# Attention ordered by blocks, with projections ending at steps and the softmax division at the outputs

## The chip, the core and the metric

The kernel runs on one core of a Trainium2 chip. The metric is the device time of one execution, in microseconds, as the median of several.

## What is computed

Two transformer blocks over 1024 tokens of width 1024: one with an mLSTM and pooling mixer and a mixture of experts, one with forgetting attention and a multilayer perceptron. The change touches the attention of the second alone:

```python
def fox_mixer(h, w_in, b_f, q_g, k_g, w_out):
    proj = h @ w_in
    q, k, v, f_pre = jnp.split(proj, [D, 2 * D, 3 * D], axis=-1)
    q = rms_norm_2(q.reshape(B, S, 16, 64), q_g)
    k = rms_norm_2(k.reshape(B, S, 16, 64), k_g)
    F = jnp.cumsum(log_sigmoid(f_pre + b_f), axis=1)
    logits = q @ k * 64 ** -0.5 + (F[t] - F[s])      # s <= t
    p = jax.nn.softmax(logits, axis=-1)
    return (p @ v) @ w_out
```

All in f32. A product that must be exact is made of three matmuls with high and low halves (`split_mm`, lines 1622 to 1624).

## The kernel before

`build` runs phases one behind the other, each a block in which every engine has a written instruction stream and semaphores join them. The phases are mixer, experts, `attention`, `fox_out` and `mlp`. In `attention` the 16 heads are done as 8 pairs. For a pair TensorE projects the normed input to q, k and v in 8 tiles of 128 tokens (`project`, bank 4, eight k of three matmuls each). Two tiles make a batch of q and k: ACT copies the rows (`rows_out`) and squares them, DVE sums (`sums`), POOL makes the root (`root`, L1905 and L1907), DVE scales (`normed`, L2162), TensorE turns (`turn_batch`, L2003), ACT and DVE split into high and low (`high_batch`, L2081 to L2083; `low_batch`, L2171 and L2173).

A head has four groups n of 256 queries, with g = n % 4; group g sees 2g + 2 tiles of keys, in g + 1 blocks b of two. For a group: `logits` on TensorE (L1958 to L1960, banks 0 to 3), `forgotten` on DVE adds the forget sums and takes the row minimum (L2130), `exp` on ACT with the row sum (L2039), `share` on POOL: reciprocal of the row sum (L1912) and the whole probabilities times it (L1914). For each block TensorE turns the probabilities (`turn_probs`, L1975, banks 5 and 6 in turn), ACT copies the high half (L2048), DVE subtracts for the low half (L2137), and TensorE weighs v with both (`weigh`, L1991 and L1992, bank 7, whose two halves serve groups in turn). `copy_out` on ACT (L2056) and `add_out` on DVE (L2144) put the output together; SP stores it once per pair (L1888).

The streams are loops over slots, one group to a slot, written by hand. In slot n TensorE makes the logits of group n + 1 and the turning and weighing of group n, with pieces of the projection of tile n + 8 between:

```python
for n in slots:
    logits(n + 1, 0); project(n, (0, 1))
    logits(n + 1, 1); project(n, (2, 3))
    turn_probs(n, 0); project(n, (4,))
    for b in range(g + 1):
        if b < g:
            turn_probs(n, b + 1); project(n, (5 + b,))
        elif g < 3: project(n, range(5 + g, KT))
        weigh(n, b)
    if batch_in(n) is not None: turn_batch(batch_in(n))
```

Eight slots before group 0 have projections alone (the fill). The banks 5 and 6 alternate over blocks and batches in the order of turning (`z_block`, `z_batch`), and a turning waits until ACT and DVE have left its bank. The weights of a pair are loaded in two halves into one tile `w_qkv` (L1864, three DMAs each); each is split by ACT (`high_weights`, L2034) and DVE (`low_weights`, L2118), and SP loads a half only when the low split of the one before is done. In the last slot of a pair ACT does one `high_weights` behind the first turned block and the other at the slot's end.

## Time and profile before

| | |
|---|---|
| median of 3 executions | 3104.9 us (3104.64 to 3107.49) |
| profiled execution | 3103.1 us, span 3101.4 us |
| busy, share of the span | PE 83%, PEld 68%, DVE 60%, ACT 40%, POOL 18% |
| mean granted TensorE clock | 0.899 |
| attention | from 1540 to 2251 us of the span |
| L1991, weighing with the high half | 81.1 us idle before it, 80.7 of them for L2137 |
| L2048, high half of the turned probabilities | 29.6 and 35.3 us idle before its two forms |

Times are of one profiled execution. PE is the matrix engine (TensorE), PEld its weight loads, DVE VectorE, ACT ScalarE, POOL GpSimd, SP the engine that issues DMAs. A clock of 1.0 is 2.4 GHz. Ends of matmuls are modelled and they overlap, so the time that a matmul takes is read from the start of it to the start of the next.

### The profile page before, as it was taken

How to read it: one execution, taken by the hardware profiler on the slowest of the kernel's cores; microseconds unless marked ns; L12 is line 12 of the kernel's file. 1: busy time of each engine (PE TensorE's matmuls, PEld its weight loads, DVE VectorE, ACT ScalarE, POOL GpSimd, SP SyncE). 2: the span in 40 equal slices, each digit the busy share in tenths (PEclk: the TensorE clock that was granted, in tenths of full speed). 3: DMA queues.
4: the chain of work that ended last, by engine and by line, in shares of the span. 5: the costliest groups of instructions: out<-in, count | busy, mean ns of one | idle time of the engine just before them, and what ended most of it. 6: DMA issues, size and time to landing. Idle time of an engine off the chain costs nothing. (4 is left out here: it accounts for less than half of the span.)

```text
span 3101.4 us, 34604 instructions
## 1 busy us (share of the span) xinstructions
PE 2564.8 (83%) x12069; PEld 2116.0 (68%) x12069; DVE 1848.8 (60%) x2460; ACT 1250.9 (40%) x1817; POOL 563.9 (18%) x609
## 2 busy tenths in 40 slices
PE   3998767556999999981478888888685999999999
PEld 2766456455887888870377777777564888888887
DVE  6873693355888888875435555555445445554554
ACT  2212531105777777772245555555422121112111
POOL 1000020111111111104225555555400000000000
PEclk8999758757999999995599999999796999999999
DMA  5683233417968799985111110110042111111111
GB/s 210 220 291 111 96 122 102 158 42 304 393 269 318 289 390 399 398 326 217 55 52 42 41 35 31 41 31 32 7 176 68 41 54 54 41 54 41 54 54 55
DMA packets 137677, 443.01 MB, mean 143 GB/s; under 512 B 15134, under 2 KB 74050, under 8 KB 124264
## 3 DMA queue, kind: packets, MB, share of 16 engines
q1 hardware_dynamic: 124140, 394.97, 34.7%
q0 software_dynamic: 8144, 27.80, 2.5%
q10 hardware_dynamic: 5292, 18.94, 1.5%
q8 instruction: 58, 0.95, 0.1%
q14 instruction: 43, 0.35, 0.0%
HBM read 384.91 MB, written 56.76 MB: 142 GB/s over the span
## 5 line engine op out<-in xcount | busy, mean ns | idle before, releaser
L1622 PE MATMUL psum<-w_high,block_hT_high 128*128 128x512 f32 x576 | 233.4, 405 | 22.8 <-DVE w_low L1328 18.0
L2428 DVE TENSOR_TENSOR x<-x,psum 128x512 f32<-128x512 f32 x256 | 172.8, 685 | 112.4 <-PE psum L1624 112.4
L1622 PE MATMUL psum<-w_qkv_high,fox_hT_high 128*128 128x384 f32 x512 | 199.8, 390 | 34.5 <-DVE w_qkv_low L2118 25.0
L1623 PE MATMUL psum<-w_low,block_hT_high 128*128 128x512 f32 x576 | 226.7, 393 | 0.0
L1624 PE MATMUL psum<-w_high,block_hT_low 128*128 128x512 f32 x576 | 226.4, 393 | 0.0
L1328 DVE TENSOR_TENSOR w_low<-w_up,w_high 128x2048 fp32r<-128x2048 f32 x72 | 161.7, 2288 | 90.0 <-ACT w_high L1322 90.0
L1622 PE MATMUL psum<-hT_high,w_mlp_in_high 128*128 128x512 f32 x512 | 200.1, 391 | 7.1 <-DVE w_mlp_in_low L2405 7.1
L1623 PE MATMUL psum<-hT_low,w_mlp_in_high 128*128 128x512 f32 x512 | 199.9, 390 | 0.0
L1624 PE MATMUL psum<-hT_high,w_mlp_in_low 128*128 128x512 f32 x512 | 199.7, 390 | 0.0
L1622 PE MATMUL psum<-w_mlp_out_high,hiddenT_high 128*128 128x512 f32 x512 | 199.2, 389 | 0.0
L1623 PE MATMUL psum<-w_mlp_out_low,hiddenT_high 128*128 128x512 f32 x512 | 199.2, 389 | 0.0
L1624 PE MATMUL psum<-w_mlp_out_high,hiddenT_low 128*128 128x512 f32 x512 | 199.2, 389 | 0.0
L1328 DVE TENSOR_TENSOR w_low<-w_gate,w_high 128x2048 fp32r<-128x2048 f32 x72 | 164.3, 2284 | 40.0 <-ACT w_high L1322 39.9
L2137 DVE TENSOR_TENSOR probsT_low<-psum,probsT_high 128x512 fp32r<-128x512 f32 (+1 forms) x160 | 98.9, 634 | 135.6 <-ACT probsT_high L2048 135.0
L1623 PE MATMUL psum<-w_qkv_low,fox_hT_high 128*128 128x384 f32 x512 | 176.8, 345 | 0.0
L1624 PE MATMUL psum<-w_qkv_high,fox_hT_low 128*128 128x384 f32 x512 | 176.6, 345 | 0.0
L1322 ACT ACTIVATE w_high<-w_gate 128x2048 fp32r<-128x2048 f32 x72 | 137.5, 1913 | 91.9 <-DMA w_gate<-in_w_expert_gate 84.2
L1991 PE MATMUL psum<-probsT_high,v_high_low 128*128 128x256 f32 x320 | 96.6, 321 | 81.1 <-DVE probsT_low L2137 80.7
L1328 DVE TENSOR_TENSOR w_low<-w_down,w_high 128x2048 fp32r<-128x2048 f32 x72 | 161.5, 2282 | 3.5 <-ACT w_high L1322 3.5
L2416 DVE TENSOR_TENSOR relu_squared<-relu 128x512 f32<-128x512 f32 x64 | 44.2, 691 | 194.2 <-ACT relu L2384 194.2
L2379 ACT ACTIVATE w_mlp_out_high<-w_mlp_out 128x2048 fp32r<-128x2048 f32 x16 | 30.7, 1917 | 319.0 <-DVE w_mlp_out L2409 319.0
L1622 PEld LDWEIGHTS psum<-w_high,block_hT_high 128*128 128x128 f32 x576 | 109.7, 190 | 58.9 <-DVE w_low L1328 32.5
(402 smaller groups left out, 6704.7 us busy)
## 6 DMA issues: line engine op xcount, KB each, us to landing
w_gate<-in_w_expert_gate SPq DMA_DIRECT2D x32, 2048.0 KB
w_up<-in_w_expert_up SPq DMA_DIRECT2D x32, 2048.0 KB, 9.1
w_down<-in_w_expert_down SPq DMA_DIRECT2D x32, 2048.0 KB, 10.4
v_aug<-in_w_ada SPq DMA_DIRECT2D x48, 512.0 KB, 4.8
expert_rows<-block_out ACTq DMA_DIRECT2D x36, 512.0 KB, 9.1
v_aug<-in_ada_w SPq DMA_DIRECT2D x32, 512.0 KB, 4.7
expert_rows<-work SPq DMA_DIRECT2D x1, 16384.0 KB, 44.1
w_mlp_in<-in_w_mlp_in SPq DMA_DIRECT2D x16, 1024.0 KB, 5.1
```

The source lines that it names most:

```text
L1322: act.activation(wh[:, par, half], raw[kind][:, half], ACT.Copy).then_inc(s_wh, 1)
L1328: dve.tensor_tensor(wl[:, par, half], raw[kind][:, half], wh[:, par, half].bitcast(F32), ALU.subtract).then_inc(s_wl, 1)
L1622: pe.matmul(out, sh, mh, start=start, stop=False)
L1623: pe.matmul(out, sh, ml, start=False, stop=False)
L1624: return pe.matmul(out, sl, mh, start=False, stop=stop)
L1991: pe.matmul(out_, v, pTh[:, y % 2, at], start=s == 0, stop=False)
L2137: dve.tensor_tensor(pTl[:, y % 2, 0:width], bank[5 + z % 2][:, 0:width], pTh[:, y % 2, 0:width].bitcast(F32), ALU.subtract).then_inc(s_lo, 1)
L2379: act.activation(w2h[:], w2[:], ACT.Copy).then_inc(s_w2h, 1)
L2416: dve.tensor_tensor(gf[:, g % 2, :], rl[:, g % 2, :], rl[:, g % 2, :], ALU.mult).then_inc(s_sq, 1)
L2428: dve.tensor_tensor(x3[:, t, at], x3[:, t, at], bank[4 + j % 4], ALU.add).then_inc(s_r, 1)
```

## The change

The streams are now loops over steps, one block to a step: 20 steps of fill and 160 blocks. In step y TensorE turns block y + 1, makes the logits of the group whose first block is y + 4, runs a share of a projection, and weighs block y. A pair's 8 tiles are cut into 18 shares of 2 to 4 k, such that a tile ends with a step; steps 18 and 19 of a pair have none. A batch whose second tile ends in step c is turned at the end of step c + 2 and split in step c + 3. Both halves of the next weights are split in step 18. The names with changed lines: logits L1988 to L1990, `turn_probs` L2009, `weigh` L2024 and L2025, `turn_batch` L2037, `high_weights` L2060, `exp` L2065, `high_probs` L2074, `copy_out` L2081, `rows_out` L2088, `high_batch` L2105 to L2107, `low_weights` L2137, `forgotten` L2149, `low_probs` L2156, `add_out` L2162 and L2164, `low_batch` L2190 and L2192.

The probabilities stay undivided. POOL makes a 128x128 diagonal of reciprocals per query tile; one matmul of ones with the two diagonals (L2029) spreads them over the partitions in the second half of bank 7, and DVE multiplies the finished output by it. The first half of bank 7 serves all groups, so a group's first weighing waits for the output before it. The semaphores are counted apart for blocks and batches, and each g has a probabilities tile of its own.

```diff
-            pe_ = sbuf(c2, "probs_even", [P, 5 * P + 6 * P])
-            po_ = sbuf(c2, "probs_odd", [P, 7 * P + 8 * P])
+            pb = [sbuf(c2, f"probs{g}", [P, (4 * g + 3) * P]) for g in range(4)]
+            dg = sbuf(c2, "recip_diagonal", [P, 2, 2 * P])
...
+            STEPS = 20
+            AHEAD = 4
+            BUSY = 18
+            parts = ((0, 4, 8), (0, 4, 8), (0, 3, 6, 8), (0, 4, 8), (0, 4, 8), (0, 3, 6, 8), (0, 4, 8), (0, 4, 8))
+            blocks = [(n, b) for n in range(NG) for b in range(n % QUADS + 1)]
...
                     def share(j):
...
-                        pool.tensor_scalar(probs(n, u), probs(n, u), rs[:, j % 4:j % 4 + 1], None, ALU.mult).then_inc(s_p, 1)
+                        if n >= 2 and u == 0:
+                            pool.wait_ge(s_rb, n - 1)
+                        pool.tensor_scalar(dg[:, n % 2, u * P:(u + 1) * P], ident[:], rs[:, j % 8:j % 8 + 1], None, ALU.mult).then_inc(s_dg, 1)
+                    for y in steps:
+                        if batch_at(y - 1) is not None:
+                            root(batch_at(y - 1))
+                        if group_at(y - 1) is not None:
+                            for u in range(2):
+                                share(2 * group_at(y - 1) + u)
...
+                    def bank_left(z):
+                        if z >= 2:
+                            kind, at = holds[z - 2]
+                            pe.wait_ge(s_hi if kind == "block" else s_bh, at + 1)
+                            pe.wait_ge(s_lo if kind == "block" else s_bl, at + 1)
...
                     def weigh(n, b):
-                        if b == 0 and n >= 2:
-                            pe.wait_ge(s_o, n - 1)
-                        pe.wait_ge(s_lo, z_block[n, b] + 1)
+                        if b == 0 and n >= 1:
+                            pe.wait_ge(s_o, n)
+                        pe.wait_ge(s_lo, y + 1)
...
+                        if b == g:
+                            pe.wait_ge(s_dg, 2 * n + 2)
+                            pe.matmul(bank[7][:, 2 * P:HALF], ones[:], dg[:, n % 2, :], start=True, stop=True).then_inc(s_rb, 1)
...
+                    for y in steps:
+                        if 0 <= y + 1 < NY:
+                            turn_probs(*blocks[y + 1])
+                        if group_at(y) is not None:
+                            logits(group_at(y), 0)
+                            logits(group_at(y), 1)
+                        for q, k in products_at(y):
+                            project(q, k)
+                        if y >= 0:
+                            weigh(*blocks[y])
+                        if batch_at(y - 2) is not None:
+                            turn_batch(batch_at(y - 2))
...
+                    for y in steps:
+                        if 0 <= y + 1 < NY:
+                            high_probs(*blocks[y + 1])
+                        if left_at(y) is not None:
+                            copy_out(left_at(y))
+                        if group_at(y - 1) is not None:
+                            exp(2 * group_at(y - 1))
+                            exp(2 * group_at(y - 1) + 1)
+                        if batch_at(y - 3) is not None:
+                            high_batch(batch_at(y - 3))
+                        if y % STEPS == BUSY and y // STEPS + 2 < PAIRS:
+                            high_weights(2 * (y // STEPS + 2))
+                            high_weights(2 * (y // STEPS + 2) + 1)
+                        if tile_at(y) is not None:
+                            rows_out(tile_at(y))
+                        if batch_at(y) is not None:
+                            square(batch_at(y))
...
                     def add_out(n):
-                        dve.tensor_tensor(o[rows[h], at], o[rows[h], at], bank[7][rows[h], half:half + 2 * P], ALU.add).then_inc(s_o, 1)
+                        dve.tensor_tensor(o[rows[h], at], o[rows[h], at], bank[7][rows[h], 0:2 * P], ALU.add).then_inc(s_oa, 1)
+                        dve.wait_ge(s_oa, n + 1)
+                        dve.tensor_tensor(o[rows[h], at], o[rows[h], at], bank[7][rows[h], 2 * P:HALF], ALU.mult).then_inc(s_o, 1)
...
+                    for y in steps:
+                        if 0 <= y + 1 < NY:
+                            low_probs(*blocks[y + 1])
+                        if left_at(y) is not None:
+                            add_out(left_at(y))
+                        if batch_at(y - 2) is not None:
+                            normed(batch_at(y - 2))
+                        if group_at(y) is not None:
+                            forgotten(2 * group_at(y))
+                            forgotten(2 * group_at(y) + 1)
+                        if batch_at(y - 1) is not None:
+                            sums(batch_at(y - 1))
+                        if batch_at(y - 3) is not None:
+                            low_batch(batch_at(y - 3))
+                        if y % STEPS == BUSY and y // STEPS + 2 < PAIRS:
+                            low_weights(2 * (y // STEPS + 2))
+                            low_weights(2 * (y // STEPS + 2) + 1)
+                        if tile_at(y) is not None:
+                            v_low(tile_at(y))
```

The order on TensorE where a batch has been turned, in the first pair: the reciprocals (`recip_diagonal`) and the batch (`qk_rows`) at the end of step 5, then step 6 with a turned block, the logits of a small group and the first k of the projection.

```order
L2029 MATMUL psum<-recip_diagonal,ones 128x256
L2037 MATMUL psum<-ident,qk_rows 128x128 x4
L2009 MATMUL psum<-ident,probs 128x128 x4
L1988 MATMUL psum<-k_high_twice,q_stacked 128x128
L1989 MATMUL psum<-k_low,q_stacked 128x128
L1990 MATMUL psum<-causal_bf,ident_bf 128x128
L1988 MATMUL psum<-k_high_twice,q_stacked 128x256
L1989 MATMUL psum<-k_low,q_stacked 128x256
L1990 MATMUL psum<-causal_bf,ident_bf 128x128
L1622 MATMUL psum<-w_qkv_high,fox_hT_high 128x384
L1623 MATMUL psum<-w_qkv_low,fox_hT_high 128x384
L1624 MATMUL psum<-w_qkv_high,fox_hT_low 128x384
```

One more k follows here and one weighing; then the next block is turned, into the batch's bank. Before, a whole slot's projection of eight k stood around two turnings.

The order on ACT at the weights of a pair, before, in the last slot of the pair before it (`w_qkv_high` is the high split):

```order
L2048 ACTIVATE probsT_high<-psum 128x512
L2034 ACTIVATE w_qkv_high<-w_qkv 128x1536
L2039 ACTIVATE probs_even,row_sum<-probs_even,row_min 128x256
L2048 ACTIVATE probsT_high<-psum 128x512 x2
L2048 ACTIVATE probsT_high<-psum 128x384
L2064 ACTIVATE qk_rows<-psum 128x256
L2065 ACTIVATE v_high_low<-psum 128x2x64
L2072 ACTIVATE qk_square<-qk_rows 128x512
L2034 ACTIVATE w_qkv_high<-w_qkv 128x1536
L2056 ACTIVATE outT<-psum 64x256
```

and now, in steps 18 and 19:

```order
L2065 ACTIVATE probs,row_sum<-probs,row_min 128x384
L2065 ACTIVATE probs,row_sum<-probs,row_min 128x512
L2060 ACTIVATE w_qkv_high<-w_qkv 128x1536 x2
L2074 ACTIVATE probsT_high<-psum 128x384
L2074 ACTIVATE probsT_high<-psum 128x512
L2081 ACTIVATE outT<-psum 64x256
L2065 ACTIVATE probs,row_sum<-probs,row_min 128x640
L2065 ACTIVATE probs,row_sum<-probs,row_min 128x768
```

The two splits were seven instructions apart and now are one row with x2; the copies of turned blocks stand behind both.

The order on DVE at the same place, before (`w_qkv_low` is the low split, `qk_rows` the scaling of a batch):

```order
L2137 TENSOR_TENSOR probsT_low<-psum,probsT_high 128x512
L2118 TENSOR_TENSOR w_qkv_low<-w_qkv,w_qkv_high 128x1536
L2130 ISA probs_even,row_min<-psum,forget_sums 128x256
L2130 ISA row_min 128x1
L2137 TENSOR_TENSOR probsT_low<-psum,probsT_high 128x512 x2
L2137 TENSOR_TENSOR probsT_low<-psum,probsT_high 128x384
L2151 TENSOR_TENSOR v_high_low<-psum,v_high_low 128x128
L2118 TENSOR_TENSOR w_qkv_low<-w_qkv,w_qkv_high 128x1536
L2130 ISA probs_odd,row_min<-psum,forget_sums 128x384
```

and now:

```order
L2156 TENSOR_TENSOR probsT_low<-psum,probsT_high 128x384
L2176 TENSOR_REDUCE qk_sums<-qk_square 128x8
L2137 TENSOR_TENSOR w_qkv_low<-w_qkv,w_qkv_high 128x1536 x2
L2156 TENSOR_TENSOR probsT_low<-psum,probsT_high 128x384
L2181 TENSOR_TENSOR qk_rows<-qk_rows,qk_sums 128x512
L2149 ISA probs,row_min<-psum,forget_sums 128x640
L2149 ISA row_min 128x1
```

Both low splits stand in one row, ahead of a turned block's subtraction and the scaling of the batch that TensorE turns at the end of step 19.

## Rows read from the trace of the kernel before

**Rows 1.** two stretches of attention; us, busy us per engine (instructions), clock, DMA share, GB/s
```profile
1776.40:1858.10 81.70, 70.46 (x434) 62.27 (x433) 45.09 (x95) 46.26 (x107) 44.03 (x40) 0.98 0.13 40
2181.60:2250.70 69.10, 45.47 (x205) 36.82 (x205) 29.09 (x61) 27.98 (x62) 35.89 (x30) 0.68 0.02 8
```

**Rows 2.** waits of TensorE in attention: us in total, times, longest
```profile
PE psum L1991 <- DVE probsT_low L2137: 80.7, 68, 2.8
PE psum L1975 <- DVE k_low L2173: 11.8, 13, 1.2
PE psum L1975 <- POOL probs_odd L1914: 1.7, 2, 1.2
```

**Rows 3.** TensorE in order of time in steady pairs: start, us, instruction
```profile
1861.51 0.47 PE L1958 MATMUL psum<-k_high_twice,q_stacked 128*128 128x512 f32 x1
...
1862.27 0.42 PE L1622 MATMUL psum<-w_qkv_high,fox_hT_high 128*128 128x384 f32 x1
...
1888.75 0.36 PE L1991 MATMUL psum<-probsT_high,v_high_low 128*128 128x256 f32 x1
...
1889.30 0.60 PE L1975 MATMUL psum<-ident,probs_odd 128*128 128x128 f32 x4
1889.65 0.42 PE L1622 MATMUL psum<-w_qkv_high,fox_hT_high 128*128 128x384 f32 x1
```

**Rows 4.** TensorE in order of time in the mixer, matmuls in plain f32
```profile
310.86 1.88 PE L549 MATMUL psum<-ucT,wq 128*128 128x512 f32 x4
312.58 1.88 PE L549 MATMUL psum<-ucT,wk 128*128 128x512 f32 x4
```

**Rows 5.** groups of instructions in attention: count, busy us, mean ns, idle before
```profile
L2137 DVE TENSOR_TENSOR probsT_low<-psum,probsT_high 128x512 fp32r<-128x512 f32 x96 | 64.7, 687 | 77.4 <-ACT probsT_high L2048 77.0
L2048 ACT ACTIVATE probsT_high<-psum 128x512 fp32r<-128x512 f32 x96 | 55.0, 589 | 29.6 <-PE psum L1975 29.4
L1907 POOL TENSOR_TENSOR qk_sums<-qk_sums,minus_half 128x8 f32<-128x8 f32 x32 | 53.6, 1674 | 2.7
L2171 DVE SCALAR_TENSOR_TENSOR q_stacked<-psum,qk_gain,q_stacked 64x256 fp32r<-64x256 f32 x64 | 30.9, 483 | 48.6 <-ACT k_high_twice L2083 48.2
L2081 ACT ACTIVATE q_stacked<-psum,qk_gain 64x256 fp32r<-64x256 f32 x64 | 30.1, 470 | 18.8 <-PE psum L2003 17.5
L2144 DVE TENSOR_TENSOR outT<-outT,psum 64x256 f32<-64x256 f32 x64 | 26.7, 417 | 4.1 <-ACT outT L2056 3.2
L2056 ACT ACTIVATE outT<-psum 64x256 f32<-64x256 f32 x64 | 24.1, 376 | 19.1 <-PE psum L1992 18.6
L2162 DVE TENSOR_TENSOR qk_rows<-qk_rows,qk_sums 128x512 f32<-128x512 f32 x32 | 22.0, 689 | 12.0 <-POOL qk_sums L1907 12.0
L2157 DVE TENSOR_REDUCE qk_sums<-qk_square 128x8 f32<-128x512 f32 x32 | 21.7, 679 | 1.4 <-ACT qk_square L2072 1.0
```

**Rows 6.** all engines in order of time, weights at the fill's end
```profile
1599.19 1.47 ACT L2034 ACTIVATE w_qkv_high<-w_qkv 128x1536 fp32r<-128x1536 f32 x1
...
1600.70 1.76 DVE L2118 TENSOR_TENSOR w_qkv_low<-w_qkv,w_qkv_high 128x1536 fp32r<-128x1536 f32 x1 [1.21 <-ACT w_qkv_high L2034]
1602.48 0.37 SPq L1864 DMA_DIRECT2D w_qkv<-in_fox_w_in  x1
...
1607.51 1.48 ACT L2034 ACTIVATE w_qkv_high<-w_qkv 128x1536 fp32r<-128x1536 f32 x1 [2.85 <-DMA w_qkv<-in_fox_w_in]
...
1609.02 1.76 DVE L2118 TENSOR_TENSOR w_qkv_low<-w_qkv,w_qkv_high 128x1536 fp32r<-128x1536 f32 x1 [4.56 <-ACT w_qkv_high L2034]
```

**Rows 7.** TensorE in order of time behind the fill
```profile
1600.38 0.23 PE L1960 MATMUL psum<-causal_bf,ident_bf 128*128 128x128 bf16 x1
1604.56 0.66 PE L1622 MATMUL psum<-w_qkv_high,fox_hT_high 128*128 128x384 f32 x1 [3.94 <-DVE v_high_low L2151]
...
1609.31 0.52 PE L1624 MATMUL psum<-w_qkv_high,fox_hT_low 128*128 128x384 f32 x1
...
1611.12 0.34 PE L1623 MATMUL psum<-w_qkv_low,fox_hT_high 128*128 128x384 f32 x1
```

More of the change, by code:

```diff
@@ L1842, in where, with group_at, left_at, products_at @@
                 return i, r // QUADS, r % QUADS
+            def group_at(y):
+                n, b = blocks[y + AHEAD] if 0 <= y + AHEAD < NY else (None, 1)
+                return n if b == 0 else None
+            def left_at(y):
+                n, b = blocks[y - 1] if y >= 1 else (None, None)
+                return n if n is not None and b == n % QUADS else None
+            def products_at(y):
+                i, c = y // STEPS + 1, y % STEPS
+                if i >= PAIRS or c >= BUSY:
+                    return []
+                t, ks = shares[c]
+                return [(TT * i + t, k) for k in ks]
+            def tile_at(y):
+                done = [q for q, k in products_at(y) if k == KT - 1]
+                return done[0] if done else None
+            def batch_at(y):
+                q = tile_at(y) if y >= -STEPS else None
+                return q // 2 if q is not None and q % 2 == 1 else None
+            z_block, z_batch = {}, {}
+            for y in steps:
+                if 0 <= y + 1 < NY:
+                    z_block[blocks[y + 1]] = len(z_block) + len(z_batch)
+                if batch_at(y - 2) is not None:
+                    z_batch[batch_at(y - 2)] = len(z_block) + len(z_batch)
+            holds = {z: ("block", y_block[nb]) for nb, z in z_block.items()} | {z: ("batch", m) for m, z in z_batch.items()}
             def probs(n, u):
                 g = n % QUADS
-                buf = po_ if g % 2 else pe_
-                width = (2 * g + 1 + u) * P
-                start = 0 if u == 0 else (7 * P if g % 2 else 5 * P)
-                return buf[:, start:start + width]
-            def batch_in(n):
-                return (n + 6) // 2 if n % 2 == 0 and 0 <= (n + 6) // 2 < NB else None
+                start = 0 if u == 0 else (2 * g + 1) * P
+                return pb[g][:, start:start + (2 * g + 1 + u) * P]
             with nc.Block() as block:
@@ L2125, in forgotten @@
                             dve.wait_ge(s_f[h], 16 * (i + 1))
[L2126 to L2127 removed]
+                        if n >= QUADS and u == 0:
+                            dve.wait_ge(s_t, z_block[n - QUADS, g] + 1)
                         dve.wait_ge(s_lg, j + 1)
```

169 lines of the change are left out of this document (41 added, 128 removed).

## The prediction

> **What bounds the kernel now.** I read the stretches of attention by head pair first [rows 1], then the waits of TensorE [rows 2], then single instructions. Attention is a stage of its own, whose last output is stored at 2250.7 us. A pair of heads takes 81.7 us and TensorE counts as busy for 70.5 of them, at a granted clock of 0.98. DVE and ACT are busy for 45 to 46, POOL for 44. So TensorE is the bound, and what it loses is waiting: 80.7 us for the low half of the turned probabilities in the whole stage, 11.8 for the low half of a batch of q and k, only 1.7 for POOL's division [rows 2]. In the last pair, which has no projections left to fill gaps, TensorE works little (clock 0.68) and the pair still takes 69.1 us [rows 1].
>
> TensorE's true work in a pair comes from starts, since busy time includes pipeline tails [rows 3]: four turned tiles 0.35 us (1889.30 to 1889.65), a weighing of four matmuls 0.55 (1888.75 to 1889.30), one chunk of logits with its mask 0.76 (1861.51 to 1862.27). One k of a projection is three matmuls at 0.17, so 0.52. A pair has 64 k (33.3), 88 transposes (7.7), 80 weighing matmuls (8.3 with the narrow ones), logits of 9.9, and 0.1 for each switch between kinds (3.8): 63 us. The other 18.7 of the 81.7 are waits.
>
> **The change, part by part.** *Removed:* POOL's pass over the probabilities. It stood on TensorE's path for 1.7 us [rows 2], so its end is worth almost nothing in the first seven pairs; in the last one it is in the chain of every group. *Added:* one matmul of 256 columns in plain f32 per group. Such matmuls show as two records each; four records, two matmuls of 512 columns, start 1.72 us before the next four [rows 4], so 0.86 for 512 columns and 0.43 for 256. With a switch I take 0.5, 8 per pair: 4 us, and TensorE's work becomes 67. The bounds are 0.43 and, at half clock, 0.95. DVE gets a second 0.42 us operation per group on the outputs [rows 5]: 3.4 us per pair on an engine with 36 free, but in the chain below. POOL's new 128x128 products are off the path.
>
> *Moved:* the order. Turned probabilities are now weighed a whole step later, with a projection between; a chain of copy 0.59 and subtraction 0.69 [rows 5] fits under that. The 80.7 us of waits go, as meant. What is late next are four other waits; I walked the 20 steps of a pair, with E the end of its last projection.
>
> 1. *Weights, once per pair.* ACT now makes the two high halves of the next weights one behind the other, and so does DVE with the low halves (the order on ACT and on DVE). They share one staging tile: the second half is loaded only after the first has been subtracted. The trace has this chain once, at the end of the fill [rows 6]: high copy at 1599.19, low at 1600.70, load issued at 1602.48, second high copy at 1607.51 after 2.85 us idle. That is 8.3 us from copy to copy, and the second low ends 3.3 later. Before, a slot's work stood between the two. Now ACT starts at E+3.0 (seven instructions stand ahead, at the mean of 0.43 us that 46.26 us for 107 give [rows 1]), the second high copy starts at E+11.3 and DVE is free at E+14.6. Behind it on DVE stand one subtraction and the scaling of the last batch, 1.3 us together. TensorE needs that scaled batch at E+4.0, after 3.5 us of other work in the two steps without projection, and gets it at E+15.9: 11.9 us.
>
> 2. *Batches, four per pair.* The two banks for turning alternate, so the second turning after a batch waits for the batch's bank. In the step between, ACT does a probabilities copy 0.59, an output copy 0.38 and six batch copies of 0.47, then DVE four of 0.48 [rows 5]: with 0.6 for the turning itself it ends 6.3 us after the step began. TensorE's work in those steps is 2.5 to 3.6 (the order on TensorE shows the shortest: 2 k, two small logits). So it waits 3 us, four times: 12.1. The nearest row is L1975 waiting 11.8 us in 13 waits for the same DVE line [rows 2]: there several pieces of projection stood between.
>
> 3. *Outputs.* One half bank is left for a group's output (the other holds the reciprocals), so the next group's first weighing waits for the store of the last: after the turning 0.3, copy 0.59, subtraction 0.69, add and multiply 0.84, some 2.5 us, against 1.1 to 2.2 of projection. Over eight groups 3.6 us.
>
> 4. *Small ones:* a projection tile that waits for the last one's copies behind a long step (0.8 and 0.9), a batch whose root (1.67 us [rows 5]) is queued on POOL behind a reciprocal that waits for an output (0.85), and one more (0.35): 2.9 us.
>
> A pair: 67 + 11.9 + 12.1 + 3.6 + 2.9 = 97.5. After the long wait TensorE runs slow: following 3.94 us idle the matmuls took 0.52 us in place of 0.34 from 1604.56 to past 1609.31 [rows 7], five microseconds that do the work of half as many, so up to 2.5 lost, part of it under wait 2. I add 2: a period of 99.5.
>
> *The sum.* Before, the fill's last matmul starts at 1600.4 [rows 7], and the end is at 2250.7: 650.3 us. After, the fill is the same, seven sets of weights each open a pair's period, and the last pair runs alone. It keeps 12 steps of 1.3 us (half the copy, subtraction and weighing chain), eight handovers of 3.7, 10 of logits that partly show, and one batch wait, 62 us; with some of it at half clock, as now (0.68), I take 66. So 7 x 99.5 + 66 = 762.5, 112 more than 650.3. The profiled execution took 3103.1 us (span 3101.4); its median is 3104.9, 1.8 higher, and I carry that along: **3217 us**.
>
> The Trainium skill (DMA: Bandwidth & Descriptors, Anatomy of one DMA) states about 2.0 us fixed plus bytes over 436 GB/s. For the 786 KB of one half of the weights that gives an estimate of 3.8 us, where the rows have 5.0 from first issue to the copy; by the page each pair would be 1.2 us shorter, 3209 in all. The measured load decides.
>
> **Rivals.**
>
> *Projections stay the bound, and it is faster.* The new order hides all the chains, and a pair is its work of 67 plus 3.6 at the outputs: 7 x 70.6 + 62 = 556, 94 less, **3011**. For it speaks that 80.7 us of waits have no place left; against it that in the order the paired weights and the bank's return stand where nothing covers them. It decides at a period of (650.3 - 66) / 7 = 83.5: all waits of a pair under 16.5 us, where I count 30.5. Chance 0.06.
>
> *The weights' load is covered.* If the second half is ready when ACT asks, 8.3 us shrink to some 1.5, seven times: 48 less, **3169**. For it: three loads of one half land quickly at times; against: the tile is single, and the load waits for DVE. Chance 0.08.
>
> *The clock falls at each wait.* If the 3 us waits lower TensorE's clock as the 3.94 us one did [rows 7], four per pair lose up to 2.5 each, less the 2 already counted: 7 x 8 = 56 more, **3273**. Against it: waits up to 2.8 us [rows 2] left the clock of a pair at 0.98 [rows 1]. Chance 0.07.
> The Trainium skill (TensorE: Matmul & The Clock Gate, HAM oscillation) states that a wait for data between bursts makes the array start each burst at the low clock; that is this rival, and it speaks against the change. The trace agrees for 3.94 us and not for 2.8.
>
> *It moves waits and nothing more:* the new waits come to the old ones, a period of 83.5, **3105**. Chance 0.03.
>
> **How the numbers follow.** My forecast has 0.76. A measurement of this kernel tells 0.2%, 6 us, from no change. The range: the nearest large uncertainties are the start of the weights chain (1 us per pair), the waits for batches (2.3 to 3.5 us each, 5 per pair) and the clock (0 to 5 per pair), together about minus 45 and plus 50 around 3217; it takes in the covered load and reaches to the clock's rival: 3150 to 3268. Outside are the faster case, the equal one and half of the clock's, 0.13. Faster by over 0.2%: 0.06. Within: 0.03. Slower: 0.76 + 0.08 + 0.07 = 0.91.
>
> **What would show it.** The waits of the weighing (L2024) for the low half near 0 outside the last pair; the turning of batches (L2037) waiting some 12 us, once per pair, for the scaling on DVE; ACT idle 3 to 5 us before each second weights copy for its DMA; L2009 waiting about 3 us for DVE's k_low, four times a pair; stores of outputs 97 to 102 us apart. I am wrong if the stores are under 84 us apart, or if L2037's waits are short: then the weights were hidden. A granted clock under 0.85 in a full pair would be the clock's rival.

## The result and the profile after

The changed kernel takes **3273.9 us** (median of 4, 3269.0 to 3279.4) against 3105.0 on the same chip: a ratio of 1.0543, 95% interval 1.0522 to 1.0563. The profiled execution took 3269.0 us (span 3267.2). The forecast was slower, 3217; the time lies 57 us above it, 6 above the range.

All of it is in attention, which ends at 2418.2 in place of 2250.7. What follows it is 850 us long in both traces. A full pair and the last one, in the columns of [rows 1]:

```profile
1946.09:2052.46 106.37, 78.17 (x442) 70.79 (x442) 48.42 (x102) 45.80 (x107) 27.07 (x41) 0.87 0.10 30
2360.50:2418.20 57.70, 37.48 (x203) 30.43 (x203) 27.64 (x58) 24.45 (x54) 13.70 (x24) 0.80 0.03 10
```

A pair grew from 81.7 to 106.4 us. TensorE's busy time grew by 7.7 and its granted clock fell from 0.98 to 0.87; DVE and ACT do what they did, POOL does 17 us less. The waits of TensorE in attention (us in total, times, longest), which stand against [rows 2]:

```profile
PE psum L2037 <- DVE qk_rows L2181: 89.5, 16, 12.9
PE psum L2009 <- DVE k_low L2192: 67.6, 22, 4.1
PE psum L2024 <- DVE outT L2164: 32.5, 29, 2.3
PE psum L2009 <- issue: 20.2, 7, 2.9
PE psum L1622 <- ACT qk_rows L2088: 17.8, 19, 1.1
...
PE psum L2024 <- DVE probsT_low L2156: 0.9, 3, 0.3
```

The 80.7 us for the low half are 0.9 now, as meant; in their place stand 210 us for batches, banks and outputs. The long wait is the weights' chain, here in all engines' order of time (against [rows 6]):

```profile
2032.80 0.33 PE L1624 MATMUL psum<-w_qkv_high,fox_hT_low 128*128 128x384 f32 x1
...
2035.81 1.48 ACT L2060 ACTIVATE w_qkv_high<-w_qkv 128x1536 fp32r<-128x1536 f32 x1
2037.33 1.76 DVE L2137 TENSOR_TENSOR w_qkv_low<-w_qkv,w_qkv_high 128x1536 fp32r<-128x1536 f32 x1 [1.52 <-ACT w_qkv_high L2060]
...
2043.73 1.48 ACT L2060 ACTIVATE w_qkv_high<-w_qkv 128x1536 fp32r<-128x1536 f32 x1 [6.44 <-DMA w_qkv<-in_fox_w_in]
2045.25 1.76 DVE L2137 TENSOR_TENSOR w_qkv_low<-w_qkv,w_qkv_high 128x1536 fp32r<-128x1536 f32 x1 [6.16 <-ACT w_qkv_high L2060]
2047.39 0.68 DVE L2181 TENSOR_TENSOR qk_rows<-qk_rows,qk_sums 128x512 f32<-128x512 f32 x1
```

From E = 2032.8: the copies start at E+3.0 and E+10.9, and TensorE goes on at 2048.22, E+15.4, after 11.01 us. The sum had 3.0, 11.3 and 15.9. What the sum had not is in the first and third of these windows of the pair, right behind two of the waits for a batch's bank (3.30 and 2.88 us long); the second stands behind one of 2.94 us:

```profile
1951.40:1956.60 5.20, 5.20 (x19) 5.20 (x20) 1.29 (x3) 1.35 (x4) 0.00 (x0) 0.50 0.00 0
1979.00:1984.00 5.00, 4.94 (x32) 4.53 (x33) 2.01 (x6) 1.91 (x6) 2.29 (x4) 1.00 0.00 0
2002.70:2007.70 5.00, 5.00 (x16) 3.79 (x17) 2.12 (x4) 0.60 (x1) 0.00 (x0) 0.50 0.00 0
```

At 0.50 (1.2 GHz) TensorE does 16 to 19 matmuls in 5 us, at 1.00 (2.4 GHz) 32. This pair is the exception: in the other five pairs before the last, the clock falls behind all four waits for a batch's bank. In the pair before this one, two windows behind the waits of 2.95 and 2.63 us:

```profile
1871.50:1874.80 3.30, 3.30 (x12) 2.78 (x11) 1.77 (x5) 1.31 (x5) 2.18 (x4) 0.50 0.02 5
1919.30:1926.00 6.70, 6.17 (x21) 5.37 (x22) 2.25 (x6) 1.59 (x5) 2.29 (x4) 0.50 0.00 0
```

I multiplied the busy time of every microsecond of a pair by one minus its clock, and call it the lost work: 9.2 us in the pair from 1946 to 2052 (7.9 to 10.1 in the five pairs that have the long wait), and 1.7 in each of four pairs of before. There the clock falls once a pair, behind a wait of some 2.0 us, while a longer one in the same pair leaves it high (kernel before; the waits, then the windows behind them):

```profile
2001.10 0.38 PE L1991 MATMUL psum<-probsT_high,v_high_low 128*128 128x256 f32 x1 [1.96 <-DVE probsT_low L2137]
2014.06 0.38 PE L1991 MATMUL psum<-probsT_high,v_high_low 128*128 128x256 f32 x1 [2.80 <-DVE probsT_low L2137]
```

```profile
2002.70:2006.00 3.30, 3.30 (x15) 3.30 (x15) 0.59 (x3) 2.49 (x8) 0.80 (x1) 0.50 0.00 0
2014.10:2018.10 4.00, 3.81 (x26) 3.46 (x27) 1.35 (x3) 2.90 (x5) 0.38 (x1) 1.00 0.46 128
```

### The profile page after: what moved, and what is told of

Same layout as the page of the kernel before. It is cut to its first block and busy times, and to the rows that moved or that the text cites. A ratio compares the mean times of both kernels' runs of the same rounds, so it can differ in the third digit from the quotient of the medians.

```text
span 3267.2 us, 34985 instructions
## 1 busy us (share of the span) xinstructions
PE 2616.3 (80%) x12197; PEld 2171.6 (66%) x12197; DVE 1877.1 (57%) x2524; ACT 1251.2 (38%) x1817; POOL 424.2 (13%) x609
## 5 line engine op out<-in xcount | busy, mean ns | idle before, releaser
L2156 DVE TENSOR_TENSOR probsT_low<-psum,probsT_high 128x512 fp32r<-128x512 f32 (+1 forms) x160 | 102.0, 638 | 239.1 <-ACT probsT_high L2074 239.1
L2074 ACT ACTIVATE probsT_high<-psum 128x512 fp32r<-128x512 f32 (+1 forms) x160 | 88.8, 555 | 361.4 <-PE psum L2009 361.3
L1623 PE MATMUL psum<-w_qkv_low,fox_hT_high 128*128 128x384 f32 x512 | 185.7, 363 | 0.0
L1624 PE MATMUL psum<-w_qkv_high,fox_hT_low 128*128 128x384 f32 x512 | 184.3, 360 | 0.0
L2009 PE MATMUL psum<-ident,probs 128*128 128x128 f32 x576 | 102.6, 302 | 87.7 <-DVE k_low L2192 67.6
```

The source lines that it names most:

```text
L1623: pe.matmul(out, sh, ml, start=False, stop=False)
L1624: return pe.matmul(out, sl, mh, start=False, stop=stop)
L2009: ins = pe.transpose(bank[5 + z % 2][:, at:at + P], probs(n, u)[:, s * P:(s + 1) * P], ident[:])
L2074: act.activation(pTh[:, y % 2, 0:width], bank[5 + z % 2][:, 0:width], ACT.Copy).then_inc(s_hi, 1)
L2156: dve.tensor_tensor(pTl[:, y % 2, 0:width], bank[5 + z % 2][:, 0:width], pTh[:, y % 2, 0:width].bitcast(F32), ALU.subtract).then_inc(s_lo, 1)
```

## The experiments

Ratios are to the kernel before on the same chip, us differences are ratio differences times 3104.

| run | ratio (95%) | against the changed kernel |
|---|---|---|
| changed kernel | 1.0543 (1.0522 to 1.0563) | |
| e1 weights split | 1.0320 (1.0303 to 1.0337) | -69 |
| e2 late | 1.0142 (1.0125 to 1.0159) | -124 |
| e3 filler in the long wait | 1.0535 (1.0517 to 1.0552) | -2 |
| e4 no division | 1.0455 (1.0435 to 1.0475) | -27 |
| e5 order alone | 1.0658 (1.0640 to 1.0676) | +36 |
| e6 division alone | 1.0104 (1.0086 to 1.0121) | -136 |
| e7 = e1 and e2 | 1.0070 (1.0053 to 1.0087) | -147 |
| e8 = e7, old division | 1.0079 (1.0061 to 1.0097) | -144 |
| e9 filler, misplaced | 1.1008 (1.0983 to 1.1032) | +144 |
| e10 second half later | 1.0167 (1.0145 to 1.0190) | -117 |
| e11 transposes late only | 1.0953 (1.0927 to 1.0979) | +127 |
| e12 filler at two banks | 1.0536 (1.0519 to 1.0554) | -2 |
| e13 copies first only | 1.0268 (1.0251 to 1.0285) | -85 |
| e14 = e7, scaling early | 1.0053 (1.0035 to 1.0071) | -152 |
| e15 = e1 and e13 | 1.0193 (1.0168 to 1.0218) | -109 |
| e16 better order | **0.9823 (0.9810 to 0.9837)** | -223 |
| e17 = e16, old division | 0.9889 (0.9874 to 0.9905) | -203 |
| e18 = e14, two stores | 0.9993 (0.9984 to 1.0003) | -171 |

**e1, the weights' halves in two steps** (ACT, and the same on DVE):

```diff
-if y % STEPS == BUSY and y // STEPS + 2 < PAIRS:
-    high_weights(2 * (y // STEPS + 2))
-    high_weights(2 * (y // STEPS + 2) + 1)
+if y % STEPS in (17, 19) and y // STEPS + 2 < PAIRS:
+    high_weights(2 * (y // STEPS + 2) + y % STEPS // 19)
```

> One thing is changed: the two halves of a pair's weights are copied and split in steps 17 and 19 of a pair instead of both in step 18, so the second half's load, which starts when the first half has been subtracted, lies beside a step and a half of other work. Theory (the long wait of TensorE once a pair, 12.9 us on qk_rows in the changed kernel, is ScalarE standing 6.7 us for that load and the two copies behind each other): the wait for DMA at the weights' copy falls from 6.7 us to under 1, TensorE's wait once a pair from 12.9 to 2 to 4 us, seven pairs, so about 60 to 70 us less with what the clock gives back: 3274 becomes about 3208. Rival (the long wait hides other waits, which appear in its place: the batch's chain of square, sums, root and product is as long by itself): TensorE still waits 8 us or more in step 19, and the time falls by under 30 us, to 3245 or more.

3201.1 us, 69 less. The waits in e1's trace:

```profile
PE psum L2009 <- DVE k_low L2191: 63.0, 22, 3.8
PE psum L2024 <- DVE outT L2163: 42.1, 35, 2.3
PE psum L2037 <- DVE qk_rows L2180: 23.0, 16, 4.0
```

The wait for scaled batches fell by 66.5 us, the outputs' rose by 9.6. ScalarE still waits for the load, 14.7 us in all in place of 45.7, so 2.1 each time where under 1 was expected. The theory holds, with its size: 9.5 us of TensorE's wait per pair came from copying and splitting both halves in one step; ScalarE's own wait for the load is 4.4 us shorter.

The pairs of e1 also show what the clock costs. TensorE has the same instructions in each and stands still for 19.8 to 20.1 us; these three lose 8.5, 6.4 and 10.0 us of work:

```profile
1713.23:1810.66 97.43, 77.63 (x440) 69.45 (x440) 48.56 (x102) 45.56 (x107) 27.48 (x40) 0.89 0.11 33
1810.66:1906.35 95.69, 75.62 (x440) 67.61 (x440) 48.52 (x102) 45.70 (x107) 27.48 (x40) 0.93 0.11 34
1906.35:2005.11 98.76, 78.95 (x440) 70.47 (x440) 48.42 (x102) 45.80 (x107) 27.49 (x40) 0.88 0.11 33
```

Between the second and the third the lost work grows by 3.6 us and the pair by 3.1: nearly all of it is paid for.

**e2, the order inside a step.** On PE:

```diff
 for y in steps:
-    if 0 <= y + 1 < NY:
-        turn_probs(*blocks[y + 1])
     ... logits, project ...
+    if 0 <= y + 1 < NY:
+        turn_probs(*blocks[y + 1])
     if y >= 0:
         weigh(*blocks[y])
```

and on ACT and DVE `high_probs` and `low_probs` move from the front of a step to behind output, exp (`forgotten`), batch and rows; the weights come last.

> The order inside a step is changed and no instruction added or taken away: TensorE issues logits and projections ahead of the transposes of the next block, and ScalarE and VectorE take batch and output work ahead of the block's copy. Theory (the four waits of about 3 us a pair on k_low and the waits for outT come from transposes that stand at the front of a step and need a bank that the batch's copies still hold; with matmuls ahead of them they are covered): those waits fall from 67.6 us and 32.5 us in all to under 20 and 10, the stretches at half clock that follow them go too, and the time falls by 80 to 140 us, to about 3135 to 3195, with the long wait for weights left as it is. Rival (the waits only change place, since ScalarE and VectorE are then late with the block's copies, which weigh needs in the same step): waits at the matmuls on probsT_low take their place and the time stays within 20 us of 3274 or rises.

124 us less. The waits on k_low fell from 67.6 us (22 times) to 2.7 (once), those of the outputs to 7.9. The waits for scaled batches rose by 20, to 109.8 us. The expectation holds. All waits of TensorE in attention together fell by some 70 us, and the work lost at half clock from about 9 to 1.4 to 3.0 us a pair, some 50 us in all: together nearly the 124. So the lost work is paid for here.

**e13 and e11, its two halves.** e13 has the edits on ACT and DVE alone, e11 the one on PE alone.

> The other half of the order inside a step: ScalarE and VectorE do output, exp and batch ahead of the next block's copy, TensorE keeps the changed kernel's order with the transposes in front. Theory (the bank wait is the batch's copies standing behind the block's copy; taking them first frees the bank and the outputs about 1.3 us earlier): the waits on k_low fall from 67.6 us by a third to a half and those on outT from 32.5 to about 10, 40 to 80 us less: 3195 to 3235. Rival (both halves are needed together, since the block's copy is now late for the weighing in the same step): as slow as 3274 or slower, with waits of the weighing on probsT_low.

> Half of the earlier run of the order inside a step: only TensorE's order is changed, logits and projections ahead of the next block's transposes; ScalarE and VectorE keep the changed kernel's order, the block's copy first. Theory (what was saved there, 127 us, came from TensorE having work to do before it needs the bank): most of it, 80 us or more, so 3195 or less. Rival (ScalarE and VectorE now stand at the block's copy, which comes later, and do the batch behind it, so the bank comes free later too): less than 40 us, 3235 or more.

e13 took 3183.3 us, 85 less, more than the 40 to 80 expected: the waits on k_low fell from 67.6 to 19.9 us. (Its edit on DVE also moves the scaling of a batch behind `forgotten`, as e2's does.) e11 took 3394.7, 127 **more**. Alone, the late transposes are waited for by ACT at the front of its step, with the last group's output behind them, so TensorE waits for the output in nearly every group (e11's trace):

```profile
PE psum L2024 <- DVE outT L2164: 130.9, 58, 3.6
```

The rival of e11 (3235 or more) was right in its number but named the wrong wait (k_low is 9.9 there). The two halves are no sum: -85 and +127 give -124 together. An order on three engines is one thing.

**e3, filler in the long wait.**

```diff
+if y % STEPS == STEPS - 1 and y // STEPS + 2 < PAIRS:
+    pe.wait_ge(s_raw, TT * (y // STEPS + 2))
+    pe.wait_ge(s_vl, TT * (y // STEPS + 2))
+    for _ in range(56):
+        pe.matmul(bank[4][:, 0:W3], hTh[:, 0, 0:P], hTh[:, 0, 0:W3], start=True, stop=True)
```

> 56 matmuls of 128x384 whose result nobody reads are added once a pair, in step 19 in front of the batch's transposes, where TensorE stands for about 11 us; they are about 9 us of work at full clock and end before what TensorE waits for there. Theory (part of the change's cost is that the clock falls to half at such a wait and the matmuls behind it run slowly): with the wait filled, the work behind it runs at full clock, and the kernel becomes 1.5 to 4 us a pair faster though it does more: about 3248 to 3264. Rival (the clock's share is nothing that this wait causes): the time stays at 3274 within 4 us, or rises.

3268.8 us, no difference. The trace is of an execution of 3282.3 us, the slowest of the four. The filler filled the wait and the clock held behind it (first row), but the next turning waits for its bank whatever TensorE does: 4.10 us, where the changed kernel has 3.30 to 4.06, and it starts 5.3 us after the pair's store in both kernels. Behind the later waits the clock fell as it does in most pairs of the changed kernel, and stayed low for longer: a pair loses 10.8 to 12.5 us. The second row is behind the wait of 2.62 us (3.1 us lost); the changed kernel lost as much there in one pair, 1.4 to 1.5 in four, and held the clock in one (the row by itself):

```profile
1944.90:1947.90 3.00, 2.79 (x19) 2.47 (x17) 2.57 (x7) 2.29 (x5) 0.31 (x1) 1.00 0.82 238
1922.60:1928.60 6.00, 6.00 (x21) 5.17 (x22) 1.86 (x5) 1.59 (x5) 2.29 (x4) 0.50 0.00 0
```

```profile
2029.30:2035.30 6.00, 5.95 (x42) 5.46 (x42) 2.71 (x8) 3.71 (x12) 2.30 (x4) 1.00 0.00 0
```

**e9, filler at the short waits, misplaced.**

```diff
+if batch_at(y - 3) is not None and y >= 0 and y % STEPS != 6:
+    done = sum(1 for x in range(-STEPS, y) if tile_at(x) is not None)
+    pe.wait_ge(s_raw, done)
+    pe.wait_ge(s_vl, done)
+    for _ in range(40):
+        pe.matmul(bank[4][:, W3:HALF], hTh[:, 0, 0:P], hTh[:, 0, 0:P], start=True, stop=True)
```

> The changed kernel with 40 matmuls of 128x128 that nobody reads put where TensorE waits some 3 us for a batch's bank, in three of the four places of a pair (in the fourth a projection tile is open in bank 4); about 2.3 us of work each at full clock. In the changed kernel TensorE is busy at half clock for 9.2 us of lost work a pair, most of it right behind these waits, and only 1.7 in the kernel before. Theory (the 7 us a pair that the sum missed are that lost work): with the clock held, 3 to 6 us a pair come back though work is added, so 3230 to 3255, ratio about 1.045. Rival (as in the run with filler in the long wait, what TensorE does faster it waits longer for at the next bank): 3268 or more, ratio 1.052 or more.

144 us more. It tests nothing of the theory: it is the second turning after a batch that waits for its bank, and the filler stood ahead of the first, where nothing is waited for. It was also twice as long as the 2.3 us that I had put for it, a third of the 0.17 of a 128x384 matmul each:

```profile
2080.90 4.66 PE L2046 MATMUL psum<-fox_hT_high 128*128 128x128 f32 x40
```

**e12, filler where the waits are.**

```diff
+if y >= 0 and y % STEPS in (1, 12):
+    pe.wait_ge(s_add, 2 * sum(1 for x in range(-STEPS, y) if group_at(x) is not None))
+    for _ in range(20):
+        pe.matmul(bank[1][:, 0:2 * P], hTh[:, 0, 0:P], hTh[:, 0, 0:2 * P], start=True, stop=True)
```

> The run before put its filler one turning too early, where TensorE does not wait, and its 128x128 matmuls start only every 0.117 us, so it was added work and no test. Here 20 matmuls of 128x256 (0.117 us each, 2.3 us) stand directly in front of the two turnings, in steps 1 and 12 of a pair, at which the changed kernel waits 3.3 and 2.9 us and after which the clock is at half for 5 to 6 us. Theory (the 7 us a pair that the sum missed are TensorE's work at half clock behind such waits): with the clock held there, 3 to 5 us a pair less, 3240 to 3255, ratio 1.044 to 1.048. Rival (what is done faster is waited for at the next bank, as in the run with filler in the long wait): 3266 or more, ratio 1.052 or more.

3267.3 us, no difference, so the rival's number; but not by its mechanism. The filler stood where it should, and the clock behind the two waits is full (windows of e12, first and third row; the changed kernel falls to 0.50 at both, in every pair):

```profile
1949.30:1954.30 5.00, 5.00 (x31) 4.54 (x32) 2.28 (x6) 2.02 (x5) 0.00 (x0) 1.00 0.00 0
1974.60:1979.60 5.00, 5.00 (x17) 4.17 (x18) 2.03 (x6) 1.58 (x5) 2.29 (x4) 0.50 0.00 0
2000.90:2005.90 5.00, 4.95 (x30) 4.27 (x31) 2.84 (x5) 0.60 (x1) 0.00 (x0) 1.00 0.00 0
2011.40:2014.60 3.20, 3.20 (x13) 3.20 (x12) 0.92 (x2) 0.00 (x0) 1.87 (x2) 0.50 0.02 5
2025.20:2028.20 3.00, 3.00 (x11) 2.17 (x12) 1.20 (x4) 1.58 (x5) 0.61 (x2) 0.50 0.00 0
```

Counted from the pair's store, the next bank's wait ends at 30.6 us in place of 32.0 to 33.0, and the wait behind the second filler ends at 64.8 in place of 66.5 to 67.5. So some 2 us come back at each: the lost work is paid for, not covered. But the clock now stays low twice as long behind the wait of 2.93 us (second row, 3.0 us lost in place of mostly 1.7), and falls in every pair behind one of 1.28 us that had left it high in all pairs but one (fourth row, 1.7 us lost). So a pair still loses 7.9 us and takes 105.8, the same as the pairs of the changed kernel that lose 7.9 and 8.0 (105.8 and 106.0). Holding the clock at some of the waits made it fall for longer at others, and the theory's 3 to 5 us never came free to be measured.

**e4, e5 and e6, the two parts of the change apart.** e4 leaves out the division by the row sums (part of the computation), e5 is the new order with the old division, e6 the old order with the new one. Their common edit, out in e4 and e5 and in in e6:

```diff
 ins.then_inc(s_pv, 1)
-if b == g:
-    pe.wait_ge(s_dg, 2 * n + 2)
-    pe.matmul(bank[7][:, 2 * P:HALF], ones[:], dg[:, n % 2, :], start=True, stop=True).then_inc(s_rb, 1)
```

> The division by the row sums is left out altogether: the diagonals on GpSimd, the matmul of ones with them and VectorE's product with its result are gone, and ScalarE's copy of the output waits for the last product with v instead. Theory: per pair 8 matmuls in float32 of about 0.5 us go (4 us), and the waits for outT (32.5 us in all) shrink by half, so 40 to 55 us less: about 3220 to 3235. Rival (what the division's matmul and product cost is covered by the other waits): the time falls by under 15 us.

> The changed kernel with the old division: GpSimd multiplies the probabilities again, the turning waits for that, and the diagonals, the matmul of ones and VectorE's second product are gone. So it is the new order of steps by itself. Theory (the order costs nearly all of the 169 us, by the weights' chain, the batches' banks and the slow clock; the division moved to the outputs costs about 4 us a pair): 3235 to 3250, near the 3242 that the kernel without any division took, since GpSimd works four blocks ahead. Rival (GpSimd's pass over the probabilities is on the path in this order): above 3255, with waits of the transposes for GpSimd.

> The kernel before with only the division moved: reciprocals as diagonals on GpSimd, one matmul of 256 columns with ones per group, the product on the outputs, and so one half of bank 7 for outputs in place of two; the order of the slots is the old one. Theory: TensorE gets 4 us more work a pair, 32 in all, and waits for the outputs of the last group that the second half of the bank used to cover; the last pair gets shorter by GpSimd's passes: 3105 plus 32 plus 10 to 30 less 5 to 10, about 3130 to 3160. Rival (it is the division that costs most): above 3200. Other rival (it gains by itself): 3105 or less.

e4 3242.2, e5 3307.8, e6 3135.6 us: e4 is 7 us above its range, e5 at its rival, e6 in its range. Without a division the new order costs 141 us (1.0455). The division at the outputs adds 27 to that, on GpSimd it adds 63: in the new order GpSimd's pass **is** on the path, with a wait that the changed kernel has not (e5's trace):

```profile
PE psum L2007 <- DVE k_low L2185: 97.8, 29, 4.6
PE psum L2032 <- DVE qk_rows L2174: 83.8, 15, 11.6
PE psum L2007 <- POOL probs L1948: 40.2, 17, 5.0
```

In the old order the new division costs 32 us, near the 8 matmuls of 0.5 us a pair; TensorE's busy time less the lost work of a full pair is 64.4 to 64.9 us in e4 and 68.3 to 69.3 in the changed kernel. So the two parts don't add: order alone +204, division alone +32, both +169.

**e7, e8, e10, e14, e15, e18: towards an order without these waits.** e7 is e1 and e2 together, e8 the same with the old division, e15 is e1 and e13 together.

> The two edits of the runs before this one together: weights in steps 17 and 19, and the transposes behind logits and projections with the batch and output work first. Theory (the two costs are separate): 3144 less the long wait's 9 to 10 us a pair, seven times, 3075 to 3090, faster than the kernel before (3105), with the granted clock of a pair at 0.95 or more. Rival (in the other order the batch's chain of square, sums, root and product fills that wait anyway): over 3110, with waits of 8 us or more of the batch's transposes for the scaling.

> The same with the old division on GpSimd, no matmul of ones. Theory: 4 us of TensorE's work a pair less and shorter chains at the outputs: 25 to 40 us under the run with the new division, about 3040 to 3060, so the division at the outputs is a loss in a good order too. Rival (with the transposes late, GpSimd's pass is on the path): equal to that run or slower.

> The run with copies first on ScalarE and VectorE and transposes in front on TensorE, with the weights split in steps 17 and 19. Theory: that run less about 60 to 70 us, since the long wait goes as it did alone (73 us less) and in the first combination by less. Rival (as in the first combination, part of the long wait stays): only 20 to 40 us less.

e7 3122.1, e8 3126.7 (not to be told apart), e15 3159.1 us. After e2 the split gave 22 us, after e13 23, alone 69. The rivals of all three were nearer in number, but the wait of 8 us that e7's rival named is not there (2.3 us in its steady pairs). I had taken the two costs as separate; why the split gives less in the better orders is not shown. e8's division on GpSimd gained none of the 25 to 40 us expected.

e10 and e14 are built on e7. Both scale a batch earlier on DVE and have three diagonals; e10 also moves the second half of the weights to the next pair's first step.

```diff
-if y % STEPS in (17, 19) and y // STEPS + 2 < PAIRS:
-    high_weights(2 * (y // STEPS + 2) + y % STEPS // 19)
+if y % STEPS == 17 and y // STEPS + 2 < PAIRS:
+    high_weights(2 * (y // STEPS + 2))
+if y > 0 - STEPS and y % STEPS == 0 and y // STEPS + 1 < PAIRS:
+    high_weights(2 * (y // STEPS + 1) + 1)
```

> Built on the run that split the weights and put the transposes late: the second half of the weights goes to the first step of the next pair, VectorE scales a batch as its second task of a step instead of its fourth, and the diagonals have three buffers, so that GpSimd's root does not stand behind a diagonal that waits for an output. In that run TensorE still waited 46.5 us for scaled batches, GpSimd 64.7 us for the matmul of ones and ScalarE 4.5 us a pair for the load. Theory (these are one chain): the waits for scaled batches fall under 20 us and a pair from 85 to 80 or 82 us, so 3085 to 3105, level with the kernel before or under it. Rival (other waits come up behind): 3115 or more.

> The run with weights split in steps 17 and 19 and everything late (3122), with VectorE's scaling moved up and three diagonals, the weights left in steps 17 and 19. Theory (in the run before it was the second half of the weights in the next pair's first step that cost 6 us of waits a pair, and the scaling and the diagonals help): 3090 to 3115. Rival (scaling earlier only delays the row minimum behind it): 3122 within 6.

e10 was worse (3152.3, where 3085 to 3105 was expected): the projection of the next pair waits for the low half, some 3 us in most pairs, with others behind it. e14 took 3116.1, just above its range (3090 to 3115) and in its rival's (3122 within 6); its interval overlaps e7's, so its two edits are not shown to help. In e14's trace ScalarE still waits for two transfers:

```profile
ACT w_qkv_high L2060 <- DMA w_qkv<-in_fox_w_in: 32.1, 7, 4.8
...
ACT outT L2081 <- DMA heads_outputs<-outT: 14.3, 5, 2.9
```

**e16, e17, e18.** Three edits on e14: the first half of the weights at the front of step 17; DVE's sums ahead of the copies of the last batch; and two stores per pair:

```diff
+sp.wait_ge(s_o, 8 * i + 4)
+sp.dma_start(o_dram[i * P:i * P + DH, :], o[rows[0], :]).then_inc(s_st[0], 16)
 for m in (2 * i + 5, 2 * i + 6): weights(m)
 sp.wait_ge(s_o, 8 * i + 8)
-sp.dma_start(o_dram[i * P:(i + 1) * P, :], o[:]).then_inc(s_st, 16)
+sp.dma_start(o_dram[i * P + DH:(i + 1) * P, :], o[rows[1], :]).then_inc(s_st[1], 16)
```

> On the last version with the weights split and everything late (3116): the first half of the weights stands at the front of step 17 instead of its end, so its second load starts some 3 us sooner; VectorE sums a batch before the copies of the batch before; the output tile is stored in two halves, one per head, with a semaphore each, so that ScalarE no longer waits some 3 us for the store of the whole tile at the next pair's first copy. Theory (what is left over the kernel before is the 2.3 us wait at step 19 with the half clock behind it, and the 2.2 us wait for outT at the next pair's start with its half clock): 4 to 5 us a pair, 3075 to 3095, under the kernel before. Rival (the 4 us of float32 matmuls a pair and scattered waits of a microsecond remain): 3100 or more, no better than before.

> The same order with the old division on GpSimd and without the matmul of ones. Theory (in this order GpSimd's passes over the probabilities are in the way, so moving the division is the part of the change that pays): slower than the run with the new division by 5 to 20 us. Rival (the matmul of ones, 4 us a pair, costs more than GpSimd's passes): faster than it by 10 to 30 us.

> The version at 3116 with one of the last one's three edits: the output tile stored in two halves, one per head. Theory (ScalarE's 3 us wait for the store, with TensorE's wait for outT and its half clock behind it, was what a pair lost at its start; the weights at the front of step 17 are worth the rest): 25 to 40 us less, 3076 to 3091. Rival (nearly all of the 68 us is the weights' and the sums' place): 3105 or more.

e16 takes **3048.5 us** (3043.7 to 3058.9), 55 less than the kernel before and below its range (3075 to 3095). In its trace, of the slowest execution, the first full pair (after one in which the clock fell for 3 us):

```profile
1700.24:1775.64 75.40, 68.40 (x441) 62.69 (x440) 48.22 (x102) 45.15 (x106) 28.44 (x40) 1.00 0.14 42
```

The same instructions as in the 106.4 us of the changed kernel, at full clock: 68.4 us busy in place of 78.2. In steady pairs (here 1672 to 2130 us of e16) no wait is longer than 2.7 us; L2027 is the weighing:

```profile
PE psum L2027 <- DVE outT L2168: 16.0, 18, 2.7
PE psum L1622 <- ACT qk_rows L2091: 10.9, 12, 1.1
```

e17, with the old division, is 20 us slower than e16, so in a good order the move of the division pays, as the expectation had it. e18 says that the two stores are worth 19 us (1.0053 to 0.9993; 25 to 40 were expected, and 3104.7 is its rival's number); the other two edits together the rest, some 50. I did not part those two.

## Why the prediction was partly right

Sign, place and order of the waits were right; the size was not, and the time fell outside the range, at the clock's rival (3273), which had been given 0.07. That it came within 1 us of that rival is partly luck: of the rival's 56 us the pairs took 50, and the fill, which no sum had, made up 5.

- **Weights, 11.9 us:** right (E+15.4 for E+15.9), and shown by e1. Only the sign "ACT idle 3 to 5 us" was off: it stands 6.4 to 6.7 us, near the 6.8 that the sum's own 8.3 less a copy of 1.5 gives.
- **Batches' banks, four of 3 us:** right: 3.30, 2.94, 2.88 and 2.63 in the pair shown, the first up to 4.06 in others.
- **Outputs 3.6 and small ones 2.9:** the pair shown has 5.3 us in such waits (0.46 to 1.28 each) where the sum had 6.5.
- **Work 67 us:** 106.4 less 28.0 of waits and 9.2 of lost work is 69.2, so 2 us more (pipeline tails and waits too short to be listed).
- **The step that failed: "I add 2", the clock.** It was 9.2 us in the pair shown and 9.1 on average over the seven periods. The sum had the clock fall behind the long wait alone; in five of six pairs it falls behind all four bank waits as well (1.4 to 3.1 us of work each), and in the pair shown behind two of them and a wait of 1.28. Seven times 7.1 us is 50 of the 55 us by which attention ended late. The argument against the rival, that waits up to 2.8 us left the clock of a pair at 0.98, took the longest wait for the one that counts: in the kernel before the clock did fall once a pair, behind a wait of 2.0, and held behind those of 2.5 to 2.8. The length of a wait alone doesn't tell. By the Trainium skill (TensorE: Matmul & The Clock Gate, HAM oscillation) waits between bursts make the bursts start slow; most of the bank waits here bear it out, though not every one, and e2 turns it round: without the short waits a pair loses 1.4 to 3.0 us. The prediction cited the page for this rival, and should have given it more than 0.07.
- **"The fill is the same":** 4.9 us off. A tile's copies on ACT and DVE now stand behind the batch's six and four, and the projection that needs its bank waited once 4.06 us:

```profile
1576.79 0.41 PE L1622 MATMUL psum<-w_qkv_high,fox_hT_high 128*128 128x384 f32 x1 [4.06 <-issue]
```

- **Last pair 66 us:** 67.0 from the last projection to the store at 2418.2. The terms named for it come to 58 with 3 us for the batch wait, not 62, so this is near by luck in part.
- **Division:** its 4 us a pair agree with e6 (+32 in all). "Its end is worth almost nothing" (POOL's pass) held for the old order only; in the new one it would have cost 36 us more than the new division (e5).
- **The clause "a granted clock under 0.85 in a full pair would be the clock's rival"** was set too low: with 0.87 the rival's price was already paid.

That the lost work is paid for, and so makes up the 50 us, rests on three things: the pairs of e1, which differ in lost work alone and grow with it; e2, where waits and lost work together give the gain; and the sum of a pair. e12 and e3 don't test it further, since with the filler the lost work of a pair did not shrink below that of the changed kernel's best pairs.

## What to carry to other kernels

An order that removes the waits of one kind must be walked for the others on all engines at once: two loads into one staging tile back to back, a bank that several copies hold, an output tile whose store is waited for. Here they cost together far more than the waits removed (210 us for 80), and with all three eased the same idea was 1.8% faster than the kernel before. Price a new wait of some 3 us on TensorE at half again to twice its length, for the half clock behind it (1.4 to 3.1 us lost behind waits of 2.6 to 4.1 here), and do not try to hold the clock with filler: take the wait away.

## What the hardware showed that was not expected

- The length of a wait does not settle whether the clock falls behind it. In six pairs of the changed kernel it fell behind waits of 2.88 every time and behind those of 2.94 and 2.63 five times; in the kernel before it fell behind waits of 2.0 and held behind one of 2.80; in e12 it fell behind one of 1.28 in every pair. What decides stays open.
- A matmul of 128x128 on these operands took as long from one to the next as one of 128x256: 40 in 4.66 us and 20 in 2.54 us, 0.12 each, while 56 of 128x384 took 10.07 us, 0.18 each. In such a run of equal matmuls narrow pieces save nothing. The kernel's own narrow ones are faster: two weighings of 128x128 take 0.17 together where two of 128x256 take 0.23 (2079.66 to 2080.06 in e9's trace), and the transposes of 128x128 of [rows 3] follow each other in 0.09.
